# Two transformer blocks on one core: the linear attention's SiLU moved tile by tile into the sparse attention

## What is computed

```python
# per head: o is the attention's output, r a projection of the same input
o = o * lax.rsqrt(jnp.mean(o * o, axis=-1, keepdims=True) + RMS_EPS) * norm_g
o = o.reshape(B, GLA_HEADS, S, GLA_DV).transpose(0, 2, 1, 3).reshape(B, S, GLA_V_W)
return o * jax.nn.silu(r)          # silu(r) = r * sigmoid(r)
```

## Time and profile before

| | us |
|---|---|
| median of 3 runs (1610.93 to 1613.65) | 1611.87 |
| the profiled execution, its own time | 1612.44 |
| span of the profiled execution in the trace | 1610.6 |
| PE busy | 1523.8 |
| POOL busy | 675.0 |
| DVE busy | 705.4 |
| ACT busy | 591.9 |
| linear attention's last matmul to the first of the sparse attention | 6.4 |

### The profile page before, as it was taken

How to read it: one execution, slowest core, us unless ns; L and a number is a source line. 1 busy time by engine, 2 the same in 40 slices (tenths; PEclk the granted TensorE clock), 3 DMA queues, 4 the chain that set the end, 5 groups by cost and what they waited for, 6 DMA issues and landing times.

```text
span 1610.6 us, 20217 instructions
## 1 busy us (share of the span) xinstructions
PE 1523.8 (95%) x7270; PEld 1180.3 (73%) x7270; DVE 705.4 (44%) x1073; ACT 591.9 (37%) x900; POOL 675.0 (42%) x318
## 2 busy tenths in 40 slices
PE   6989999899999896999999997999989999999998
PEld 5778777566668684888888885766557888888887
DVE  5212244466653557433333124888846433333001
ACT  4122323554554224322323223565554323323221
POOL 2333412382223345444444445565413444444443
PEclk9989999899999997999999998999999999999999
DMA  3622311111112221333333332422112333333333
GB/s 137 157 85 66 92 52 39 28 52 53 53 51 81 79 82 47 94 91 96 100 92 104 105 105 79 143 66 66 53 40 66 105 91 100 95 93 102 104 105 105
DMA packets 48900, 135.03 MB, mean 84 GB/s; under 512 B 12724, under 2 KB 17080, under 8 KB 48840
## 3 DMA queue, kind: packets, MB, share of 16 engines
q1 hardware_dynamic: 39504, 130.56, 27.2%
q10 hardware_dynamic: 9336, 3.64, 1.0%
HBM read 132.09 MB, written 2.10 MB: 83 GB/s over the span
## 4 chain that ended last, share of the span: by engine, by line
PE 76%; issue 11%; DVE 6%; POOL 5%; ACT 2%; DVEq 0%; POOLq 0%; ACTq 0%
PE bank L965 19%; PE bank L966 18%; PE bank L967 18%; PE bank L994 3%; POOL wL L403 3%; PE bank L996 2%; PE bank L995 2%; PE bank L1218 1%; PE bank L1220 1%; PE bank L1219 1%; DVE tmp L1729 1%; PE bank L1150 1%; DVE bank L1813 1%; PE bank L1184 1%; PE bank L1169 1%
## 5 line engine op out<-in xcount | busy, mean ns | idle before, releaser
L403 POOL TENSOR_TENSOR wL<-raw,wH 128x1024 fp32r<-128x1024 f32 x235 | 570.4, 2428 | 877.9 <-ACT wH L491 694.0
L491 ACT ACTIVATE wH<-raw 128x1024 fp32r<-128x1024 f32 x209 | 221.2, 1059 | 710.6 <-PE bank L967 643.4
L965 PE MATMUL bank<-aH,wH 128*128 128x512 f32 x1056 | 424.0, 402 | 49.0 <-DVE aL L1456 28.2
L966 PE MATMUL bank<-aL,wH 128*128 128x512 f32 x1056 | 417.2, 395 | 0.0
L967 PE MATMUL bank<-aH,wL 128*128 128x512 f32 x1056 | 417.0, 395 | 0.0
L965 PEld LDWEIGHTS bank<-aH,wH 128*128 128x128 f32 x1056 | 202.0, 191 | 109.6 <-issue 41.9
L966 PEld LDWEIGHTS bank<-aL,wH 128*128 128x128 f32 x1056 | 202.7, 192 | 42.0 <-issue 1.2
L967 PEld LDWEIGHTS bank<-aH,wL 128*128 128x128 f32 x1056 | 202.0, 191 | 42.7
L965 PE MATMUL bank<-fH,wH 128*128 128x512 f32 x352 | 137.2, 390 | 0.0
L967 PE MATMUL bank<-fH,wL 128*128 128x512 f32 x352 | 137.0, 389 | 0.0
L966 PE MATMUL bank<-fL,wH 128*128 128x512 f32 x352 | 137.0, 389 | 0.0
(11 more groups left out here) (263 smaller groups left out, 1851.6 us busy)
## 6 DMA issues: line engine op xcount, KB each, us to landing
raw<-in_w SPq DMA_DIRECT2D x235, 512.0 KB, 3.5
bmk<-in_bias SPq DMA_DIRECT2D x6, 512.0 KB, 4.8
pj<-in_x SPq DMA_DIRECT2D x4, 512.0 KB, 6.8
out_x<-z2T SPq DMA_DIRECT2D x8, 256.0 KB, 3.6
ct<-in_ct ACTq DMA_DIRECT2D x3, 384.0 KB, 3.6
w1k<-in_w1k ACTq DMA_DIRECT2D x2, 512.0 KB, 6.1
w1v<-in_w1v ACTq DMA_DIRECT2D x2, 512.0 KB, 9.1
pv<-in_pv ACTq DMA_DIRECT2D x1, 128.5 KB, 5.9
```

Source lines behind the costliest of these rows:

```text
L403: pool.tensor_tensor(wL[:, c_slot, :], raw[:, c_slot, :], wH[:, c_slot, :].bitcast(F32), ALU.subtract).then_inc(sem("w_lo"), 1)
L491: act.activation(wH[:, s, :], raw[:, s, :], ACT.Copy).then_inc(sem("w_hi"), 1)
L965: pe.matmul(bank[:], hi, H[:, ka, :], start=(k == 0), stop=False)
L966: pe.matmul(bank[:], hi, L[:, ka, :], start=False, stop=False)
```

## The change

The one SiLU over eight tiles and the two loads of function tables around it go. In their place each r tile is treated by itself within the sparse attention, at steps (0,2) to (0,8) and (1,1) (the table `SIGMOID_AT`): ACT forms sigmoid(r) as exp(-ln(1 + exp(-r))) in the buffer `tmp`, after `over_sums` of that step, and DVE multiplies the r tile by it at the end of its own part of that step; POOL waits for each tile (`r_silu`) just before it multiplies it with the head's output. The logarithm and the exponent of `rs4` move behind `over_sums` of steps (0,0) and (0,1), `queries(0)` comes right after the linear attention, and PE waits for each of the banks that the linear attention held where it first writes it, not for all of them at the start.

```diff
+        SIGMOID_AT = {(0, 2): 0, (0, 3): 1, (0, 4): 2, (0, 5): 3, (0, 6): 4, (0, 7): 5, (0, 8): 6, (1, 1): 7}
...
-            pool.wait_ge(sem("r_silu"), 1)
...
                     linked(pool.tensor_tensor(o, o, rs, ALU.mult))
+                    pool.wait_ge(sem("r_silu"), 2 * h + e + 1)
                     pool.tensor_tensor(r_, o, r_, ALU.mult).then_inc(sem("gla_fin"), 1)
...
-            act.wait_ge(sem("bank_free"), NBANK + PH["mgn"].t0)
-            act.activation(pj[:, GRR:GRR + KD, :], pj[:, GRR:GRR + KD, :], ACT.Silu).then_inc(sem("r_silu"), 1)
-            act.preload_act_table_set("natural_log_exp_and_others")
-            act.wait_ge(sem("gla_head"), GH + 1)
-
             def queries(r):
                 act.activation(qst[:, r % 2, :], pj[:, NQ + r, :], ACT.Copy, scale=DH ** -0.5 * 2.0 ** r).then_inc(sem("nsa_q"), 1)
             queries(0)
-            act.activation(rs4, bT[:], ACT.Ln).then_inc(sem("gla_rs"), 1)
-            act.wait_ge(sem("gla_rs"), 1)
-            act.activation(rs4, rs4, ACT.Exp, scale=-0.5).then_inc(sem("gla_rs"), 1)
+
+            def root_of_heads(n):
+                act.wait_ge(sem("gla_head"), GH + 1)
+                if n == 0:
+                    act.activation(rs4, bT[:], ACT.Ln).then_inc(sem("gla_rs"), 1)
+                    return
+                act.wait_ge(sem("gla_rs"), 1)
+                act.activation(rs4, rs4, ACT.Exp, scale=-0.5).then_inc(sem("gla_rs"), 1)
+
+            def sigmoid_of_r(n):
+
+                s_ = tmp[:, n % 2, :]
+                act.wait_ge(sem("bank_free"), NBANK + PH["mgn"].t0)
+                if n >= 2:
+                    act.wait_ge(sem("r_silu"), n - 1)
+                act.activation(s_, pj[:, GRR + n, :], ACT.Exp, scale=-1.0).then_inc(sem("r_act"), 1)
+                act.wait_ge(sem("r_act"), 2 * n + 1)
+                act.activation(s_, s_, ACT.Ln, bias=1.0).then_inc(sem("r_act"), 1)
+                act.wait_ge(sem("r_act"), 2 * n + 2)
+                act.activation(s_, s_, ACT.Exp, scale=-1.0).then_inc(sem("r_sig"), 1)
...
                 if j:
                     over_sums(r, j)
+                if r == 0 and j < 2:
+                    root_of_heads(j)
+                if (r, j) in SIGMOID_AT:
+                    sigmoid_of_r(SIGMOID_AT[r, j])
...
-            pe.wait_ge(sem("gla_head"), GH + 1)
...
+            pe.wait_ge(sem("bank_free"), NBANK + PH["mgn"].t0)
             for s in range(len(NSTEPS) + 2):
                 if s < len(NSTEPS):
                     scores(*NSTEPS[s])
+                    if s == 0:
+                        pe.wait_ge(sem("gla_raw"), GH)
+                    if s == 1:
+                        pe.wait_ge(sem("gla_head"), GH + 1)
                     gate_products(M_UNITS[NSTEPS[s][1]][0])
...
                     gate_over_sum(r, j)
+                if (r, j) in SIGMOID_AT:
+                    n = SIGMOID_AT[r, j]
+                    dve.wait_ge(sem("r_sig"), n + 1)
+                    dve.tensor_tensor(pj[:, GRR + n, :], pj[:, GRR + n, :], tmp[:, n % 2, :], ALU.mult).then_inc(sem("r_silu"), 1)
```

## The result

The changed kernel takes 1623.06 us as the median of six runs (1622.83 to 1624.42), the kernel before 1611.74 beside it (1610.88 to 1613.65): a ratio of 1.007, 95% interval 1.006 to 1.0081, so 11.3 us slower. The profiled execution took 1622.83 us with a span of 1621.0. 1625 was predicted, with a range of 1614 to 1635.

The account below looks back on a forecast made before the run. The prediction took PE, busy for 95% of the span, as the bound. Its terms, -6.4 - 2.5 + 10.0 + 7.7 + 1.9 + 2.3, gave +13.0 us on 1612.4: 1625, range 1614 to 1635.

Parts of the forecast that it names:

- the closed chain: In each sigmoid step DVE's product waits for ACT and the next maxima stand behind it, so neighbouring steps do not overlap.
- The gain at the start: At scores (0,2): PE's wait of 6.4 us goes and 2.5 comes from the clock, 8.9 us gained.
- The closed step: Steps (0,2) to (0,8): 5.8 us at widths 256 and 128, 6.9 at 384 and 512; 45.0 against PE's 35.0, loss 10.0.
- The root's exponent: ACT's exponent for the root stands before the exponentials of (0,2), on the chain, and costs 1.9 us.
- POOL's hold: POOL's operations hold DVE's `gsc` and new product, between 0.78 and 1.56 us a step; taken as 1.1, 7.7 for seven steps.
- The earlier chunks cost nothing: POOL's weight chunks before the last wait inside stretched steps: nothing, or up to 3.7 us each if the stretch were shorter.
- The part after (1,0): From (1,0) to the maxima of (1,2): 11.8 us instead of 8.5, reduced for overlap to 2.3 us lost.
- The clock: Rival: PE's waits in the steps and at tile 2 lower its clock, 0 to 7 us more, centred on 1634; chance 0.15.
- PE's scores from (0,2) to (1,0) between 50 and 56 us: Sign expected in the profile after: this distance on PE takes 50 to 56 us instead of 34.96.
- hidden, and faster: Rival: PE still sets the pace in the sigmoid steps, only the gain of 8.9 us is left, 1603.5; chance 0.10.

Follow-up runs that it names:

- pool_chunk_first: The changed kernel with POOL taking the weight chunk before it waits for the second r tile of each head; 1618.3 us.
- no_newton: The changed kernel without POOL's four Newton operations per head that refine the reciprocal root; 1624.2 us.
- one_activation: The changed kernel with ACT forming only exp(-r), the logarithm and second exponential left out, so the gate is not computed; 1617.7 us.
- product_a_step_later: The changed kernel with DVE's product at the end of the step after its sigmoid, POOL's order as changed; 1628.8 us.
- no_product: The changed kernel without DVE's product of r with its sigmoid; ACT's three activations stay and POOL waits for them; 1617.4 us.
- spread_and_later: The changed kernel with sigmoids in every second step, DVE's product behind the next step's maxima, and seven weight chunks ahead of POOL's waits; 1613.6 us.
- no_sigmoid: The changed kernel with an empty sigmoid table: no sigmoid, no product, no wait of POOL for r tiles; 1609.1 us.

## Why the prediction was right, and where it was not

The time fell 2 us under the forecast. The direction and its main reason, the closed chain, were right; that the sum came so near is partly luck, since its errors lie on both sides: against the 13.0 us of the forecast the closed steps were 2.7 less and the part after (1,0) 1.2, the hold was 1.4 more and the clock 1.5, near the stage's 11.7. By its own steps:

- **The gain at the start**, 8.9 us at scores (0,2): measured 9.0. No wait, clock at 1.00 from 294 to 316 us. Right.
- **The closed step**, 5.8 and 6.9 by width, 45.0 in all: right in kind, 2.7 too long. The changed kernel's 53.15 less its hold of 9.1 are 44.1. Two other kernels say the same: 47.8 - 4.0 is 43.8 (pool_chunk_first), and 50.7 - 4.7 of hold - 2.2 of waiting for PE is 43.8 (no_newton). The root's exponent is 1.8 of it (steps (0,2) and (0,6) without hold, 7.17 and 5.40), which leaves 42.3. By width the steps are 5.4 at 256, 6.2 to 6.3 at 384, 6.5 at 512 and 5.95 at 128. That ACT's part is on the chain in full shows in one_activation: 46.3 - 9.5 of hold - 2.2 of waiting is 34.6, 9.2 less for 9.1 taken away.
- **POOL's hold**, 7.7 us: undersized. It was 9.1 in the changed kernel, 1.30 a step, and all of it on the chain. I had reckoned that POOL waits for tiles and so holds less. But what it waits for is DVE's product, so its chunk runs behind it, over DVE's next `gsc`.
- **The earlier chunks cost nothing**: right for PE's waits in these steps, wrong for what the chunks do to DVE. PE waited 4.46, 2.20 and 1.42 us for them, and its clock fell behind the first. No maxima were late for it: the scores of (0,5) end at 319.3 and their maxima begin at 321.94, behind the product. But the same three chunks held `gsc` for 4.2 us, which is in the term above, and moving the chunk made the seven steps 5.3 us shorter through the hold alone. The condition that I had written down, that they would cost something if the stretch were shorter, came true in no_newton and one_activation (2.17 us each in step (0,5)) and in product_a_step_later.
- **The part after (1,0)**, +2.3: measured 360.93 - 351.39 = 9.54 for 8.5, so +1.1. This term was too large by 1.2. The one long wait for `wL` in step (1,2) is there, 3.45 us.
- **The clock**: it fell twice, after the waits of 4.46 and 3.45 us, and was short by 1.7 us each time. I had left that to a rival. The first spell lay where DVE set the pace; the second makes the step from 10.2 late at 365.16 to 11.7 at the end. I had argued that waits of about a microsecond leave the clock alone; pool_chunk_first, with none over 2.3 us, lost 5.1. The Trainium skill, page "TensorE: Matmul & The Clock Gate", section "HAM oscillation — how this bites in real kernels", says that waits between bursts of matmuls can take the clock down each time; the runs agree more than I gave it credit for.
- **PE's scores from (0,2) to (1,0) between 50 and 56 us**: they took 344.16 - 297.51 = 46.65. The number was DVE's; PE runs up to a step ahead of it, so the two distances differ. A slip in what to look at, without effect on the sum.
- **The rival "hidden, and faster", 1603.5**: with POOL's list as it stands it could not have come. With no sigmoid at all the kernel takes 1609.1, because POOL needs 12.1 us for what PE passes in 10.0. I had read POOL's 29.77 us of 34.96 as "little room" and not asked what happens to it when PE starts earlier.

On the hold there was a rule on record: page "SBUF — State Buffer" of the Trainium skill, section "Who interferes with whom". The trace agrees with it for the new product too: 0.69 us alone, and 1.15, 1.71 and 1.69 us where POOL was in one of its operations, with a mean of 692 ns once the Newton operations were gone. The hold of 1.30 a step lies between the 1.1 that I took and the upper bound of 1.56 to which the rule pointed.

What stays open: how the 7.3 us between no_product and the changed kernel split into DVE's wait itself, POOL's hold and the chunks, since each changes the others and the clock. And several kernels have runs that lie 6 to 8 us apart (no_product 1612.73 to 1620.96, spread_and_later 1609.58 to 1616.11), the fastest one 2.5. The mean granted clock of these runs goes with their time, from 0.979 down to 0.970 in no_product and from 0.981 down to 0.975 in spread_and_later, so spells of low clock that come in one execution and not in the next are the likely cause. What brings them, and how much of the 5.7 us of product_a_step_later they are, no run here shows.

## What to carry to other kernels

When an engine off the path does two jobs in one list, and one job gets a new wait, the other job must be costed too, and on two paths. Here the weight chunk behind POOL's wait for DVE came late for PE, which cost time only where PE or a short chain set the pace, and all four times it ran when DVE reached its next `gsc`, which it held. Moving a product off its chain without moving the chunk made the kernel slower, moving both took away the whole loss. Before one books a gain at the start of a stage, one asks of every engine that feeds it whether it starts earlier too, and how long its own list takes against the pace of the bound engine; spreading the new work over twice the steps and filling the feeder's waits with its own other work then kept 8.4 of the 9.0 us.

## What the hardware showed that I had not expected

The length of a single wait does not tell whether PE's clock falls. It stayed at 1.00 after 2.20 and 1.42 us in the changed kernel, and fell after 1.71 in no_sigmoid (0.50 from 342 to 344 us) and after 1.95 in pool_chunk_first. Two kernels with nearly the same four waits for `wL` (4.46, 2.20, 1.42 and 3.45 us; 3.62, 1.85, 1.43 and 3.46) were short of 3.4 and of 10.9 us of clock. Of the four kernels with the shortest stages three lost none, and these do all of the new work; the fourth, no_sigmoid, lost 1.7.

A held DVE instruction is drawn out in the trace, and not shifted: `gsc`, two numbers a partition, has durations from 0.16 to 2.31 us in the changed kernel, and the ones held by a chunk end within 0.02 us of its end (317.06 and 317.04, 332.82 and 332.80, 346.53 and 346.52). So such a hold does not appear in the waits of DVE, and can be taken for work.
